# Three output projections: from float32 matmuls to three passes of rounded floats, operands split on ScalarE and VectorE

## The reference, cut to what matters

```
o = causal_block_attention(...)                       # latent attention, 8 heads of 128
h = h + einsum('blf,fd->bld', o.reshape(.., 1024), w_o)          # 272 x 1024 by 1024 x 1024

out = concatenate([o_a, o_b], -1) @ w_out                        # 256 x 1536 by 1536 x 1024
x = x + rmsnorm_2(out, ng[3])

out = (y * g) @ w_o                                              # 256 x 1024 by 1024 x 1024
x = x + rmsnorm_2(out, ng[3])
```

## Time and profile before

| | |
|---|---|
| median of 3 runs | 2145.78 us (2142.66 to 2146.49) |
| profiled execution, its own time | 2144.16 us |
| its span, first to last instruction | 2142.2 us |
| TensorE busy | 1894.7 us, 88% |
| TensorE weight loads busy | 1460.0 us, 68% |
| VectorE busy | 980.9 us, 46% |
| ScalarE busy | 553.3 us, 26% |
| mean granted TensorE clock | 0.902 |
| loads | 404.26 MB, mean 189 GB/s |

### The profile page before, as it was taken

The page is one execution under the profiler, slowest core; times in us unless marked ns, Lnnn a source line. Parts: engine busy times, 40 slices in busy tenths (PEclk is TensorE's granted clock), DMA queues, the critical chain, the costliest instruction groups (busy, mean ns, idle before and its releaser), DMA issues. The chain is left out here.

```text
span 2142.2 us, 32799 instructions
## 1 busy us (share of the span) xinstructions
PE 1894.7 (88%) x14260; PEld 1460.0 (68%) x14260; DVE 980.9 (46%) x1867; ACT 553.3 (26%) x819; POOL 25.5 (1%) x16
## 2 busy tenths in 40 slices
PE   4999999889998799989974899989996997768998
PEld 3544466664443699968863489979995876537997
DVE  6122243232221666523475165556565256636564
ACT  3000012111000533312231153344332221015332
POOL 0000000000000100000000010000000000001000
PEclk8689999789998899999976999999998998589999
DMA  6799960359999555324210345535550411034540
GB/s 282 304 419 425 424 271 12 123 216 388 425 424 425 202 179 195 134 79 178 99 40 0 118 165 192 194 118 179 195 178 28 162 52 68 4 117 159 195 158 20
DMA packets 57991, 404.26 MB, mean 189 GB/s; under 512 B 6352, under 2 KB 7760, under 8 KB 10224
## 3 DMA queue, kind: packets, MB, share of 16 engines
q1 hardware_dynamic: 57840, 402.07, 49.0%
HBM read 400.99 MB, written 1.05 MB: 188 GB/s over the span
## 5 line engine op out<-in xcount | busy, mean ns | idle before, releaser
L1640 PE MATMUL ps<-ffn_xh,ffn_wh 128*128 128x256 f32 x1408 | 405.3, 288 | 28.5 <-DVE ffn_xl L1755 28.5
L1641 PE MATMUL ps<-ffn_xl,ffn_wh 128*128 128x256 f32 x1408 | 403.8, 287 | 0.0
L1642 PE MATMUL ps<-ffn_xh,ffn_wl 128*128 128x256 f32 x1408 | 403.6, 287 | 0.0
L1731 DVE TENSOR_TENSOR ffn_wl<-w,ffn_wh 128x2048 fp32r<-128x2048 f32 (+1 forms) x136 | 304.3, 2237 | 15.9 <-ACT ffn_wh L1697 14.6
L1640 PEld LDWEIGHTS ps<-ffn_xh,ffn_wh 128*128 128x128 f32 x1408 | 275.9, 196 | 31.1 <-DVE ffn_wl L1731 29.5
L1641 PEld LDWEIGHTS ps<-ffn_xl,ffn_wh 128*128 128x128 f32 x1408 | 275.9, 196 | 1.6
L1642 PEld LDWEIGHTS ps<-ffn_xh,ffn_wl 128*128 128x128 f32 x1408 | 275.6, 196 | 0.0
L1697 ACT CAST ffn_wh<-w 128x2048 fp32r<-128x2048 f32 (+1 forms) x136 | 247.1, 1842 | 18.4 <-PEq L2151 8.2
L1738 DVE TENSOR_TENSOR ffn_zg<-ps,rs 128x256 f32<-128x256 f32 x88 | 37.4, 425 | 248.5 <-PE ps L1642 248.3
L1711 ACT ACTIVATE ffn_sil<-ffn_zg 128x256 f32<-128x256 f32 x88 | 36.8, 418 | 420.3 <-DVE ffn_zg L1738 420.2
L1640 PE MATMUL ps<-ffn_wh,ffn_hidh 128*128 128x512 f32 x352 | 137.4, 390 | 0.0
(11 more groups left out here) (466 smaller groups left out, 2670.2 us busy)
## 6 DMA issues: line engine op xcount, KB each, us to landing
w<-in_ffn_gu SPq DMA_DIRECT2D x88, 1024.0 KB, 4.9
w<-in_moe_gu SPq DMA_DIRECT2D x78, 1024.0 KB, 15.3
w_extra<-in_moe_gu SPq DMA_DIRECT2D x50, 1024.0 KB, 19.8
w<-in_ffn_dn SPq DMA_DIRECT2D x44, 1024.0 KB, 4.8
w_extra<-in_moe_dn SPq DMA_DIRECT2D x32, 1024.0 KB, 17.6
w<-in_moe_dn SPq DMA_DIRECT2D x32, 1024.0 KB, 19.8
w<-in_ab_xbc SPq DMA_DIRECT2D x6, 1024.0 KB, 4.8
w<-in_ab_out SPq DMA_DIRECT2D x6, 1024.0 KB, 4.8
```

What stands on the lines that cost most here:

```text
L1640: nc.tensor.matmul(out, wh, xh, start=start, stop=False)
L1641: nc.tensor.matmul(out, wh, xl, start=False, stop=False)
L1642: return nc.tensor.matmul(out, wl, xh, start=False, stop=stop)
L1731: nc.vector.tensor_tensor(low[:, s, at], S.buf(units[n])[:, at], high[:, s, at], ALU.subtract).then_inc(*w_split.one())
```

## The change

In all three projections both operands are split into a rounded high part and a rounded remainder, and each float32 matmul is replaced by three matmuls of the rounded type: high by high, high weight by activation remainder, weight remainder by activation high.

In the latent projection a new function `project_heads` takes the place of `Linears`. ScalarE rounds the weights by half units (1024 columns, first half for k = 0 to 3, second for k = 4 to 7) and the eight tiles of `mla_oT`, VectorE makes the remainders, three units' worth of split weights are held (`parts = 3`). VectorE also still adds to `h`, now between remainders. A unit is freed when its second half is split.

In `project_joined` VectorE's copy of a transposed bank becomes a rounding copy on ScalarE, followed by a subtraction on VectorE that reads the same bank. Weights are split row by row (1024 columns), the first four rows in turn with the feature tiles, four rows are held (`parts = 4`). The matmuls now go by feature tile, with the last two tiles done token tile by token tile. A transpose bank is given back, and a feature tile is ready, at VectorE's subtraction.

```diff
-        Linears(K, [Linear("b_w_o", lambda k: oT[:, k], lambda m, ps: ..., T=L1)]).run()
+        project_heads(K, oT)
+def project_heads(K, oT):
...
+        for u in range(n):
+            S.free(units[u], w_split.at(2 * u + 2))
...
+            for m in range(KT):
+                u, odd = divmod(m, 2)
+                for k in range(HEADS):
+                    if m == 0:
+                        pe.wait_ge(*x_split.at(k + 1))
+                    if odd == 0 and k % 4 == 0:
+                        pe.wait_ge(*w_split.at(2 * u + 1 + k // 4))
+                    w = slice(k * 256 + odd * P, k * 256 + (odd + 1) * P)
+                    high, low = wh[:, u % parts, w], wl[:, u % parts, w]
+                    nc.tensor.matmul(K.ps[:, m, 0:L1], high, oh[:, k], start=k == 0, stop=False)
+                    nc.tensor.matmul(K.ps[:, m, 0:L1], high, ol[:, k], start=False, stop=False)
+                    mm = nc.tensor.matmul(K.ps[:, m, 0:L1], low, oh[:, k], start=False, stop=k == HEADS - 1)
+                mm.then_inc(*made.one())
...
+            round_half(0, 0)
+            for k in range(HEADS):
+                nc.scalar.copy(oh[:, k], oT[:, k]).then_inc(*x_high.one())
+            round_half(0, 1)
+            for u in range(1, n):
+                for j in range(2):
+                    round_half(u, j)
...
+            remainder(0, 0)
+            for k in range(HEADS):
+                dve.wait_ge(*x_high.at(k + 1))
+                nc.vector.tensor_tensor(ol[:, k], oT[:, k], oh[:, k], ALU.subtract).then_inc(*x_split.one())
+            remainder(0, 1)
+            for j in range(2):
+                remainder(1, j)
+            for u in range(2, n):
+                store(2 * u - 4)
+                store(2 * u - 3)
+                for j in range(2):
+                    remainder(u, j)
+            for m in range(2 * n - 4, KT):
+                store(m)
 def project_joined(K, turn, place, n, name, gain):
-            S.free(units[u], unit_done.at(u + 1) if u < n // 2 - 1 else post.made.at(2))
+            S.free(units[u], w_split.at(2 * u + 2))
...
+            def add(f, t, half):
+                out, tok, w = K.ps[:, 4 + 2 * t + half, :], slice(t * P, (t + 1) * P), slice(half * 512, (half + 1) * 512)
+                s = f % parts
+                nc.tensor.matmul(out, fh[:, f, tok], wh[:, s, w], start=f == 0, stop=False)
+                nc.tensor.matmul(out, fl[:, f, tok], wh[:, s, w], start=False, stop=False)
+                return nc.tensor.matmul(out, fh[:, f, tok], wl[:, s, w], start=False, stop=f == n - 1)
+            for f in range(n - 2):
+                pe.wait_ge(*taken.at(f // 2 + 1 if n > KT else n // 2))
+                pe.wait_ge(*w_split.at(f + 1))
...
+            pe.wait_ge(*w_split.at(n))
+            for t in range(2):
+                for f in (n - 2, n - 1):
+                    for half in range(2):
+                        mm = add(f, t, half)
+                mm.then_inc(*post.made.one())
...
+            round_row(0)
+            for m in range(n // 2):
+                act.wait_ge(*made.at(m + 1))
+                to = place(fh, m)
+                nc.scalar.copy(to, turned(to, m)).then_inc(*f_high.one())
+                if m < 3:
+                    round_row(m + 1)
+            for f in range(4, n):
+                round_row(f)
...
-                nc.vector.tensor_copy(to, K.ps[:, m % 4, :].rearrange("p (j t) -> p j t", j=to.shape[1])).then_inc(*taken.one())
+                dve.wait_ge(*f_high.at(m + 1))
+                to = place(fl, m)
+                nc.vector.tensor_tensor(to, turned(to, m), place(fh, m), ALU.subtract).then_inc(*taken.one())
+                if m < 3:
+                    remainder(m + 1)
+            for f in range(4, n):
+                remainder(f)
```

More of the change, by code:

```diff
@@ L1211, in mla, with sb, _, round_half @@
                  "q_made", "qsq_made", "q_summed", "q_rooted", "cqn_made", "fill_taken_v", "qr_made")
-        Linears(K, [Linear("b_w_o", lambda k: oT[:, k], lambda m, ps: nc.vector.tensor_tensor(K.h[:, m], K.h[:, m], ps, ALU.add), T=L1)]).run()
+        project_heads(K, oT)
+def project_heads(K, oT):
+    nc, S = K.nc, K.stream
+    parts, half_unit, n = 3, UNIT // 2, KT // 2
+    with ExitStack() as ctx:
+        def sb(label, shape):
+            return ctx.enter_context(nc.sbuf_tensor(label, shape, F32R))
+        oh, ol = sb("mla_oh", [P, HEADS, L1]), sb("mla_ol", [P, HEADS, L1])
+        wh, wl = sb("w_o_h", [P, parts, UNIT]), sb("w_o_l", [P, parts, UNIT])
+        units = [S.take("b_w_o", u) for u in range(n)]
+        x_high, x_split, w_high, w_split, made = K.sig("x_high"), K.sig("x_split"), K.sig("w_high"), K.sig("w_split"), K.sig("lin_made")
+        for u in range(n):
+            S.free(units[u], w_split.at(2 * u + 2))
+        halves = [slice(0, half_unit), slice(half_unit, UNIT)]
+        block = ctx.enter_context(nc.Block())
+        @block.sync
+        def _(sp):
+            S.advance(sp)
+        @block.tensor
+        def _(pe):
+            for m in range(KT):
[11 more added lines that the diff above has]
+                mm.then_inc(*made.one())
+        @block.scalar
+        def _(act):
+            def round_half(u, j):
+                act.wait_ge(*S.arrived(units[u]))
+                if u >= parts:
+                    act.wait_ge(*made.at(2 * (u - parts) + 2))
+                nc.scalar.copy(wh[:, u % parts, halves[j]], S.buf(units[u])[:, halves[j]]).then_inc(*w_high.one())
+            round_half(0, 0)
[5 more added lines that the diff above has]
+                    round_half(u, j)
+        @block.vector
+        def _(dve):
+            def remainder(u, j):
+                dve.wait_ge(*w_high.at(2 * u + j + 1))
+                nc.vector.tensor_tensor(wl[:, u % parts, halves[j]], S.buf(units[u])[:, halves[j]], wh[:, u % parts, halves[j]],
+                                        ALU.subtract).then_inc(*w_split.one())
+            def store(m):
+                dve.wait_ge(*made.at(m + 1))
+                nc.vector.tensor_tensor(K.h[:, m], K.h[:, m], K.ps[:, m, 0:L1], ALU.add)
+            remainder(0, 0)
[12 more added lines that the diff above has]
+                store(m)
@@ L2150, in project_joined, with sb @@
     nc, S = K.nc, K.stream
+    parts = 4
     with ExitStack() as ctx:
-        feat = ctx.enter_context(nc.sbuf_tensor(f"feat_{K.next()}", [P, n, SEQ], F32))
-        made, taken, unit_done = K.sig("tile_made"), K.sig("tile_stored"), K.sig("unit_done")
+        def sb(label, shape):
+            return ctx.enter_context(nc.sbuf_tensor(f"{label}_{K.next()}", shape, F32R))
+        fh, fl = sb("feat_h", [P, n, SEQ]), sb("feat_l", [P, n, SEQ])
+        wh, wl = sb("out_wh", [P, parts, D]), sb("out_wl", [P, parts, D])
+        made, f_high, taken = K.sig("tile_made"), K.sig("x_high"), K.sig("tile_stored")
+        w_high, w_split, row_done = K.sig("w_high"), K.sig("w_split"), K.sig("unit_done")
         units = [S.take(name, u) for u in range(n // 2)]
@@ L2169, in _ @@
                 turn(m).then_inc(*made.one())
[L2171 to L2177, removed]
-                for t in range(2):
[L2179 to L2185, removed]
-            pe.wait_ge(*taken.at(n // 2))
+            def add(f, t, half):
[7 more added lines that the diff above has]
+                pe.wait_ge(*w_split.at(f + 1))
+                for t in range(2):
+                    for half in range(2):
+                        mm = add(f, t, half)
+                mm.then_inc(*row_done.one())
+            pe.wait_ge(*taken.at(n // 2))
+            pe.wait_ge(*w_split.at(n))
+            for t in range(2):
+                for f in (n - 2, n - 1):
+                    for half in range(2):
+                        mm = add(f, t, half)
+                mm.then_inc(*post.made.one())
             post.tensor(pe)
@@ L2190, in _, with round_row @@
         def _(act):
+            def round_row(f):
+                act.wait_ge(*S.arrived(units[f // 2]))
+                if f >= parts:
+                    act.wait_ge(*row_done.at(f - parts + 1))
+                nc.scalar.copy(wh[:, f % parts], rows(f)).then_inc(*w_high.one())
+            round_row(0)
[7 more added lines that the diff above has]
+                round_row(f)
             post.scalar(act)
@@ L2194, in _, with remainder @@
         def _(dve):
+            def remainder(f):
+                dve.wait_ge(*w_high.at(f + 1))
+                nc.vector.tensor_tensor(wl[:, f % parts], rows(f), wh[:, f % parts], ALU.subtract).then_inc(*w_split.one())
+            remainder(0)
             for m in range(n // 2):
-                dve.wait_ge(*made.at(m + 1))
-                to = place(feat, m)
-                nc.vector.tensor_copy(to, K.ps[:, m % 4, :].rearrange("p (j t) -> p j t", j=to.shape[1])).then_inc(*taken.one())
+                dve.wait_ge(*f_high.at(m + 1))
[5 more added lines that the diff above has]
+                remainder(f)
             post.vector(dve)
```

2 lines of the change are left out of this document (added).

## The result

| | before | after |
|---|---|---|
| median of 20 runs each | 2148.88 us | 2138.02 us |
| lowest to highest | 2141.31 to 2162.38 | 2131.05 to 2149.09 |
| ratio, 95% interval | | 0.995 (0.9936 to 0.9965) |
| span of the profiled execution | 2142.2 us | 2134.7 us |
| mean granted clock | 0.902 | 0.898 |

The kernel is faster, by 0.5%. The spans differ by 7.5 us. The ratio says 10.7 us of 2148.88, with an interval from 7.5 to 13.8.

The account below looks back on a forecast made before the run. TensorE was taken to bound the kernel, each stage a chain of operands ready, streaming, then norm or addition. Gains of 1.2 (latent) + 7.3 (joined) - 1.0 (time mix) = 7.5 us gave median 2138.3 us, range 2133 to 2144.

Parts of the forecast that it names:

- rival (a): All three stages: starts hidden and the clock stays high, gain 11.5 us, profile 2134.3 us; chance 0.14.
- Streaming: All three projections: three passes save 0.078 us per 272-column and 0.176 us per 512-column float32 matmul, 19.0 us in all.
- Latent start: Latent projection: TensorE starts 2.8 us later and halts once for the second half's remainder; gain taken as 1.2 us.
- the template: The feed-forward start, whose split timings (VectorE remainder 1.23 us) were used to place the latent start.
- Joined start: Joined projection: matmuls start at about 1182.0 instead of 1181.28, then stream without halt; gain taken as 7.3 us.
- The lower end: Joined projection: if the clock rises 3.4 us later it costs 1.6 us, leaving a gain of 6.5 us.
- The alternative by which transposes do not count for the clock: Joined projection: clock rises some 5.7 us into the matmuls, gain 5.4 us, time 2140.2 us; chance 0.05, inside the forecast's.
- Time mix: Time mix projection: start delayed 4.65 us, and slow clock after a 5.5 us pause; loss taken as 1.0 us.
- The expert layer: Behind the latent stage: its loads, freed earlier, move with that stage; costed at zero, at worst eating the 1.2 us.
- rival (d): Expert layer: its loads take back the latent stage's gain, leaving 6.3 us, 2139.5 us; chance 0.04.
- (c): New stages: clock stays at 1.2 GHz while they stream, slower; 2166 us if the whole joined stage is slow; chance 0.05.
- (b): All starts: longer splits and late clock rises eat most of it; gain under 4.3, near 3 us, 2142.8 us; chance 0.17.

Follow-up runs that it names:

- e4: The whole change, but the time mix splits row 0, then all feature tiles, then rows 1 to 7; ratio 0.9914 to the kernel before, time mix stage 27.32 us.
- e10: As e9, with six short float32 matmuls, result thrown away, ahead of the latent product; median 2131.88 us, ratio 0.9911 to the kernel before.
- e5: The whole change, with six thrown-away float32 matmuls filling the pause before the time mix product; ratio 0.9941 to the kernel before, time mix stage 31.89 us.
- e3: The kernel before with only the time mix projection in three passes; ratio 1.0004 to the kernel before, time mix stage 32.42 us.
- e7: The whole change without the joined projection's third pass, all splits still done; ratio 0.9923 to the kernel before, joined stage 28.15 us.
- e12: The whole change without the latent product's two remainder passes, all splits still done; ratio 0.987 to the kernel before, latent stage 18.40 us.
- e1: The kernel before with only the latent projection in three passes; ratio 0.9986 to the kernel before, latent stage 30.40 us.
- e9: The whole change with e4's and e6's edits, and row 1 behind the second feature tile in the joined stage; median 2134.74 us, ratio 0.993 to the kernel before.
- e6: The whole change, but latent units are split by output tile instead of by k halves; ratio 0.9954 to the kernel before, latent stage 29.66 us.
- e8: The whole change, but latent weight units are freed when their tiles are made, not when split; ratio 0.9966 to the kernel before, expert layer 264.31 us.
- e11: The whole change once more, unchanged, on the same chip as e9 and e10; median 2141.39 us, ratio 0.9954 to the kernel before.

## Why the prediction was right

Forecast 2138.3 us (2133 to 2144), measured median 2138.02; spans 7.5 us apart, as the sum says. The course was right: streaming gains about 19 us and the starts take back about half. The exactness is luck. All three terms came out higher than forecast, and the gain by the ratio, 10.7 us, is nearer to rival (a)'s 11.5 than to the 7.5 of the sum. The mean stages give 10.5: latent 33.35 to 31.52 (three and seven profiles) 1.8, joined 46.94 to 38.58 (three and eight) 8.4, time mix 33.03 to 32.76 (three and seven) 0.3. The 1.8 of the latent stage can't be followed further: latent stage and expert layer together took 297.5 us before and 297.7 on the mean of the same seven. Without it the stages give 8.7, and both sums lie inside the ratio's interval. The difference of 3 us from the forecast does not show in the median, since the 20 runs of before have a median 3.1 us above that of the three runs from which I started.

- **Streaming.** Right. 0.127 and 0.2275 us a matmul: a tile took 3.02 us against 24 x 0.127 = 3.04; a joined row at two passes 1.81. From the first matmul to the second norm step the joined stage gained 8.6 us (forecast 8.4), the time mix on the fast clock (e4) 27.77 - 22.10 = 5.7 (forecast 5.6). By the Trainium skill's four passes (FP8 and Floating Point Precision, TensorE Precision Notes) three would have taken 2.75 us for a tile; the trace has 3.02.
- **Latent start.** Right in place, 2.7 us for 2.8, and one halt. The halt was 0.60 us rather than 1.6: the eight input remainders took 2.90 us, less than the template's, so the next remainder ended 6.3 us behind ScalarE's start, not 6.9 to 7.1, and the other 0.2 is the time in which the last matmul ahead of the halt finished. The term of 1.2 was a middle between 2.3 and 0; the profiles show both ends, 3.0 and 0.3, and a mean of 1.8.
- **Joined start.** The first matmul came 5.44 us behind the first transpose, 0.30 us later than before where I had set 0.72; the clock was up at the latest 6.2 us into the stage, as before. I had taken 7.3 as a middle of 8.1 and 6.5; it was 8.4. The lower end supposed a clock rise 3.4 us later, for which I had no row, and no profile shows one: in the stages with the new form it came 3.3 to 6.2 us in. The alternative by which transposes do not count for the clock did not happen: in e10 the clock rose 3.4 us into the stage with nothing but transposes running. The Trainium skill (TensorE: Matmul & The Clock Gate, PE-mode transpose) says that transposes in transpose mode don't count; if these run in that mode, which no row tells, it and the rows differ.
- **Time mix.** The delay (first matmul 8.1 us behind the first transpose, for 8.8) and the slow clock behind the pause are as forecast, in all seven profiles, and e4 and e5 show both causes apart. In four of the seven the clock had risen before the pause and fell in it; in e3, e7 and e12 it had not risen yet. The term's sign was wrong: a loss of 1.0 forecast, a gain of 0.3 on the mean. Against the old stage's good case, 32.25, the new one does lose 0.5; but the old stage has its own slow case, 34.58 in e1, which the one profile of before did not show.
- **The expert layer.** Costed at zero; e12 shows that it follows the stage. Its length scatters by more than the latent term, and 2 us for the early frees, which would be rival (d), are not excluded.
- **Rivals.** (c) did not come: no stage stayed slow longer than 5.4 us into its 512-column matmuls, nor longer than 9.7 us into those of 272 columns. (a) is what the joined stage did, alone. (b) is wrong in the joined stage and about right in the other two, which e1 and e3 can't tell from no change.

## What to carry to other kernels

When a product is made cheaper by splitting its operands, count the streaming gain per matmul and then, apart from it, the delay of the first one and what that pause does to the clock; in a stage of 30 us the start decides. Put what the first product needs at the head of both splitting engines' queues: the reorder of a few lines brought the time mix to 27.3 us (e4, e9) or 29.4 (e10), from 32.8 on the mean, more than the three-pass form had gained in that stage. Where the clock's pattern scatters by 2 us a stage, compare stages over several profiles, and test a suspected absorption with a shift much larger than the scatter.

## What the runs showed of the hardware

- The same latent code took 30.40, 30.41, 30.40, 30.41 us or 33.06, 33.03, 32.94 us, by the moment at which the granted clock rose (about 6 or 12.5 us into the stage). With the halves by tile a rise at 9.1 (e9) gave a time between: 30.96, against 29.66 at 6.2 (e6).
- In the pause of 4.5 to 4.6 us between the transposes and the matmuls of the time mix the clock fell in all four profiles in which it had risen before (after, e6, e8, e11), and in three (e3, e7, e12) it stayed down. With a pause of 1.40 us it stayed up in e4 and e9; in e10 it had not risen and came 9.5 us into the stage.
- Transposes alone can bring the clock up: 3.4 us into the joined stage of e10, 3.6 us into the time mix of e4. They don't always: in the time mixes of e1, e3, e7, e10 and e12 it was still down after all 16.
- ScalarE's rounding and VectorE's subtraction cost the same on eight strided pieces of 128 columns as on 1024 in a row (ScalarE 1.04 us, VectorE 1.22 us on the mean, both ways).
